# A second scalar operand for GpSimd's weight scalings in a two-block transformer kernel

## What is computed

```python
# swa: sliding window of 128 with sinks
e = jnp.exp(s - m)
p = e / (jnp.sum(e, axis=-1, keepdims=True) + jnp.exp(sk - m))
return jnp.einsum('bhgqk,bkhd->bqhgd', p.astype(v.dtype), vb)
...
# na: neighbourhood attention, 8 heads of 64, all 512 keys with a bias
s = jnp.einsum('brqhd,brkwhd->bhrqkw', q, k).astype(jnp.float32) + bias.astype(jnp.float32)
p = jax.nn.softmax(s.reshape(b, NA_HEADS, rows, GRID_W, kh * GRID_W), axis=-1)
...
# ca: cross attention, 4 heads of 128, 256 keys of a memory
s = jnp.einsum('bthd,bmhd->bhtm', q, kv[:, :, 0]).astype(jnp.float32)
p = jax.nn.softmax(s, axis=-1).astype(zq.dtype)
```

## Time and profile before

| | us |
|---|---|
| median of 3 runs | 2685.29 |
| the profiled execution, its own time | 2683.39 |
| its span | 2681.2 |
| PE busy | 2519.5 (94%) |
| DVE busy | 1330.3 (50%) |
| ACT busy | 715.8 (27%) |
| POOL busy | 1772.3 (66%) |

### The profile page before, as it was taken

One profiled execution on the slowest core, in us unless ns is written; L12 is line 12 of the kernel. 1 busy time (PEld: TensorE's weight loads), 2 busy tenths in 40 slices (PEclk: granted clock), 3 DMA queues, 4 the chain that ended last, 5 costly groups with the idle time before them and its releaser, 6 DMA issues. The chain is left out here.

```text
span 2681.2 us, 36597 instructions
## 1 busy us (share of the span) xinstructions
PE 2519.5 (94%) x11854; PEld 2038.9 (76%) x11854; DVE 1330.3 (50%) x2616; ACT 715.8 (27%) x1504; POOL 1772.3 (66%) x993
## 2 busy tenths in 40 slices
PE   8998889899999979899998999999999899999998
PEld 6786677588888767688886777777877777787877
DVE  6467886443342575411223566664138334751552
ACT  4305785301101263300112222222016232100002
POOL 4465455577777576577775544455779767687884
PEclk9998999999999989999999999999999999999999
DMA  7682001264563202233332311212423214233332
GB/s 262 188 232 72 1 1 39 94 206 153 176 194 94 63 17 91 74 98 94 96 100 71 102 56 57 62 56 66 108 83 71 82 50 123 79 105 91 89 104 75
DMA packets 420545, 259.73 MB, mean 97 GB/s; under 512 B 62844, under 2 KB 411513, under 8 KB 414017
## 3 DMA queue, kind: packets, MB, share of 16 engines
q1 hardware_dynamic: 395024, 199.47, 25.7%
q10 hardware_dynamic: 25393, 58.63, 6.6%
HBM read 253.86 MB, written 8.10 MB: 98 GB/s over the span
## 5 line engine op out<-in xcount | busy, mean ns | idle before, releaser
L677 POOL TENSOR_TENSOR W<-RAW,zeros 128x1024 fp32r<-128x1024 f32 (+2 forms) x349 | 668.2, 1915 | 657.8 <-PE PA L778 312.8
L684 POOL TENSOR_TENSOR W<-RAW,W 128x1024 fp32r<-128x1024 f32 (+2 forms) x355 | 849.1, 2392 | 49.2 <-ACT W L1543 19.4
L775 PE MATMUL PA<-H,W 128*128 128x512 f32 x1288 | 506.0, 393 | 7.7 <-DVEq L2412 2.3
L778 PE MATMUL PA<-H,W 128*128 128x512 f32 x1288 | 503.4, 391 | 0.0
L775 PE MATMUL PA<-A,W 128*128 128x512 f32 x944 | 373.9, 396 | 16.5 <-DVE A L2038 10.7
L778 PE MATMUL PA<-A,W 128*128 128x512 f32 x944 | 371.8, 394 | 0.0
L786 PE MATMUL PA<-H,W 128*128 128x512 f32 x1288 | 318.3, 389 | 0.0
L775 PEld LDWEIGHTS PA<-H,W 128*128 128x128 f32 x1288 | 242.3, 188 | 62.4 <-POOL W L677 7.4
L778 PEld LDWEIGHTS PA<-H,W 128*128 128x128 f32 x1288 | 242.4, 188 | 50.5 <-issue 0.5
L786 PEld LDWEIGHTS PA<-H,W 128*128 128x128 f32 x1288 | 241.7, 188 | 50.3
L786 PE MATMUL PA<-A,W 128*128 128x512 f32 x944 | 236.7, 393 | 0.0
(11 more groups left out here) (375 smaller groups left out, 3929.8 us busy)
## 6 DMA issues: line engine op xcount, KB each, us to landing
AD<-in_ada_w_dram ACTq DMA_DIRECT2D x40, 1024.0 KB, 5.1
RAW<-in_w_in_dram SPq DMA_DIRECT2D x160, 256.0 KB, 3.1
RAW<-in_mlp_w_up_dram SPq DMA_DIRECT2D x128, 256.0 KB, 3.0
RAW<-in_mlp_w_down_dram SPq DMA_DIRECT2D x128, 256.0 KB, 3.0
RAW<-in_w_up_dram SPq DMA_DIRECT2D x88, 256.0 KB, 3.1
RAW<-in_nsa_w_in_dram SPq DMA_DIRECT2D x40, 256.0 KB, 4.1
RAW<-in_w_down_dram SPq DMA_DIRECT2D x16, 384.0 KB, 3.4
RAW<-in_swa_w_in_dram SPq DMA_DIRECT2D x20, 256.0 KB, 3.3
```

The lines of the kernel that those rows point to most:

```text
L677: e.tensor_tensor(W[0][:, s, 0:kc], RAW[:, s, 0:kc], zeros[:, 0:1].rearrange("p (a b) -> p a b", b=1).broadcast_to([P, kc, P]), ALU.add).t ...
L684: e.tensor_tensor(W[1][:, s, 0:kc], RAW[:, s, 0:kc], W[0][:, s, 0:kc].bitcast(F32), ALU.subtract).then_inc(w_split, 1)
L775: pe.matmul(PA[s][:, 0:n], W[0][:, s, k], hi, start=(k == 0), stop=False)
L778: mm = pe.matmul(PA[s][:, 0:n], W[0][:, s, k], lo, start=False, stop=False)
```

## The change

Two instructions on GpSimd take another form; nothing else is touched, and no instruction is moved in any engine's order.

1. The scalings without a gate (`swa`, `na`, `ca`) multiply by the reciprocal and then by a second scalar operand, a column of the constant `ones`.
2. The high halves of the panels that are made between the scalings of `na` and `ca` (16 panels) are made by a `tensor_scalar` that adds a zero column twice as scalar operands, in place of the `tensor_tensor` addition of a broadcast column. The panels outside keep the `tensor_tensor`.

```diff
-        def split_hi(e, p, s, kc):
+        def split_hi(e, p, s, kc, filling=False):
             if not isinstance(p, int) or p >= 2:
                 e.wait_ge(w_hi_used, p - 1)
             e.wait_ge(w_loaded[s], ((p - s) * 16) + 32 if not isinstance(p, int) else (p // 2 + 1) * 32)
+            if filling:
+                e.tensor_scalar(W[0][:, s, 0:kc], RAW[:, s, 0:kc], zeros[:, 0:1], zeros[:, 0:1], ALU.add, ALU.add).then_inc(w_hi, 1)
+                return
             e.tensor_tensor(W[0][:, s, 0:kc], RAW[:, s, 0:kc], zeros[:, 0:1].rearrange("p (a b) -> p a b", b=1).broadcast_to([P, kc, P]),
                             ALU.add).then_inc(w_hi, 1)
...
                 elif grp["gate"] is None:
-                    pool.tensor_scalar(w, w, inverse, None, ALU.mult).then_inc(sem("scaled"), 1)
+                    pool.tensor_scalar(w, w, inverse, ones[:, 0:1], ALU.mult, ALU.mult).then_inc(sem("scaled"), 1)
...
                 if fills and i % plan.fill == plan.fill - 1:
-                    split_hi(pool, *fills[i // plan.fill])
+                    split_hi(pool, *fills[i // plan.fill], filling=True)
```

## The result

| | before | after |
|---|---|---|
| median of the runs | 2685.36 us (6 runs) | 2695.96 us (6 runs) |
| lowest and highest | 2681.62, 2686.85 | 2693.65, 2699.52 |
| profiled execution, its own time | 2683.39 | 2694.41 |
| its span | 2681.2 | 2692.2 |

The ratio is 1.0047, 95% interval 1.0036 to 1.0058: about 12.6 us slower (10.6 by the two medians, which lies inside the interval). The forecast was 2692.7 us, 7.4 slower, within 2681 to 2696. The direction was right, but the loss is larger than the sum: the median of 2695.96 is just inside the range, and 2685.3 x 1.0047 = 2697.9 us is above it.

What follows compares the result with a forecast made beforehand. The prediction took a loop of DVE and ACT to set `na`'s pace, with POOL beside it. Collisions +8.7 and tail -1.3, all else 0, gave +7.4 us: 2692.7 us, range 2681 to 2696.

Steps and rivals of the forecast that it cites:

- the tail: End of `na`: PE no longer waits for the last scaling; -1.3 us, bounds 0 to -2.
- Scalings at 0.77 us: The 112 scalings take 0.77 us instead of 1.87, which cuts 35 us of POOL's time in `na`.
- rival C: Second operand leaves scalings at 1.87 us, or `split_lo` stays where it is; nothing moves, 2685 us; chance 0.10.
- `split_lo` collides, 1.65 us per head: In `na`, `split_lo` starts 0.17 us before the queries' subtraction and blocks it, in six heads; +8.7 us in all.
- High halves: took 1.5 us, priced at 0: 16 high halves between scalings take 1.5 us, bounds 1.5 to 3.7; POOL done before the reciprocal in `na`; 0.
- rival D: PE's 2.3 us gap per head in `na` lets its clock fall; 1 us a head, 2699 us; chance 0.07.
- The first collision: First of six in `na`: only 0.4 us, since `split_lo` no longer holds up the bias by 1.25 us.
- `ca` and `swa` at 0: PE's waits there are not for POOL; 0 each, bounds -0.5 to +0.5 (`ca`), -0.5 to 0 (`swa`).
- Rival B: No collision in `na`: `split_lo` comes after the second keys' subtraction has begun, or DVE goes first; 2682 us, chance 0.17.

Runs made afterwards that it cites:

- the experiment on forms: Kernel before, with four forms of the scaling by turns in `swa` and three of the high half in `ca`; one execution 2682.72 us.
- halves by ones: Changed kernel with its high halves by two multiplications with ones instead of two additions of zero; 2692.23 us, ratio 1.0033 against the kernel before.
- the kernel with both parts and the wait: Changed kernel with `split_lo` in `na` waiting for the low half of the next head's keys; 2685.14 us, ratio 1.0004 against the kernel before.
- the kernel with the wait: Kernel before with the quick scalings, and `split_lo` in `na` waiting for the low half of the next head's keys; 2684.31 us, ratio 0.9991.
- the early `split_lo`: Kernel before with only `split_lo` in `na` moved one unit earlier, behind the scaling of unit 4h; 2697.40 us, ratio 1.0035.

## Why the forecast came out as it did

| part of `na`, us | before | scalings only | the change | forecast, difference |
|---|---|---|---|---|
| to head 1's queries | 6.76 | 7.78 | 7.79 | 0 |
| to head 2's | 10.45 | 10.53 | 10.53 | 0 |
| to head 3's | 12.06 | 12.74 | 13.58 | +0.4 |
| to head 7's | 47.76 | 54.23 | 56.46 | +6.6 |
| to the output projection | 24.81 | 24.38 | 26.46 | +0.35 |

(Heads are counted from 0; the forecast's five times 1.65 us are four in the fourth row and one in the last, there less the tail's 1.3. The differences of the change are +1.0, +0.1, +1.5, +8.7 and +1.7 us.)

- **Scalings at 0.77 us**: right, so rival C is out, and with them POOL's relief, though not its size. The window of the changed kernel's `na` (columns as in the earlier trace rows) has POOL busy for 72.59 of 104.5 us, where 88.30 of 93 stood and about 50 were forecast; the slow high halves take the rest. PE is busy for as long as before. That the relief buys PE nothing was read rightly from the earlier trace rows.

```profile
2002.00:2106.50 104.50, 86.36 (x486) 72.34 (x485) 88.24 (x163) 60.31 (x132) 72.59 (x47) 0.98 0.24 56
```

- **`split_lo` collides, 1.65 us per head**: right for the part that it was worked out for. The scalings alone lose 6.47 us over four heads, 1.62 each, in the subtraction and with the lead (0.20 us) that were named. For the Trainium skill (SBUF — State Buffer, § Who interferes with whom) this is the rule of the exclusive lock. For `tensor_tensor` the rows here agree: the subtraction grew from 0.69 to 2.75 us beside one of 2.40.
- **High halves: took 1.5 us, priced at 0.** This is the step that failed. It rested on the row of the gated scalings, two multiplications, as if the number of scalar operands made them quick; the experiment on forms shows that the operations do. At 3.81 us the half ends behind the reciprocal of unit 4h. The forecast said in its bounds what then follows: at 3.7 us `split_lo` comes to lie in the first subtraction for the keys, "with a loss like the one counted". That happened (2082.93, inside 2082.35 to 2083.5), yet the loss is larger than the one counted, by 0.55 us per head over four heads (8.70 instead of 6.47). The second keys lose to `split_lo` what the queries lost with the scalings alone (2.73 us instead of 0.69), and two scalings now lie beside the queries and the first keys as well. With the halves come 5.2 us of `na`'s +13.0: 0.8 in head 2, 2.2 in the four heads, and 2.1 in the last row, of which 1.6 are the clock (rival D, below). The bounds were worked out, but the upper one was then put at no cost in the sum, and the range ended at the forecast mechanism with the quick half.
- **The first collision (+0.4) and the tail (-1.3)**: with the scalings alone the first is +0.68. The last row is -0.43 where +0.35 was expected: head 7's collision costs 1.72 us (from the queries' start to the mask step 4.24 instead of 2.52), so the tail gives 2.15, more than its bound of 2. Against that stands 1.0 us at the start of `na` that nobody forecast (last section). That the scalings alone cost 7.8 us in `na`, near the sum of 7.4, is therefore partly luck.
- **`ca` and `swa` at 0**: right for `ca`; `swa` is 0.8 us shorter in the profiled execution, where 0 to 0.5 was allowed.
- **Rival B** would have needed `split_lo` behind the keys. Held there by a wait, the kernel gives 0.9991 where B had 2682 us. There the keys' subtractions take their bare 1.38 us and PE's waits for them 1.5 us in all, as B had it; B's condition was not met by the change.
- **Rival D** had the clock follow the longer gaps, at 1 us in each of six heads. The changed kernel has six gaps of 2.0 to 2.9 us. Behind five of them PE goes on at the higher level, and `na` was granted 0.98 on average, as before. Behind the last, in head 7, the clock fell: from 2086 to 2090 it shows 0.68. PE there, in the changed kernel and then with the scalings alone, where it did not fall:

```profile
2086.30 0.50 PE L1001 MATMUL PS<-KK1h,QS 128*128 128x512 f32 x1 [2.90 <-DVE KK1l L1965]
2086.87 2.25 PE L803 MATMUL PA<-H,W 128*128 128x512 f32 x6
```

```profile
2083.72 0.50 PE L998 MATMUL PS<-KK1h,QS 128*128 128x512 f32 x1 [0.82 <-DVE KK1l L1962]
2084.29 1.55 PE L800 MATMUL PA<-H,W 128*128 128x512 f32 x6
```

From these scores to the next PE takes 4.92 us (2086.30 to 2091.22) against 3.34 (2083.72 to 2087.06), and DVE then waits 0.92 us for PE. So D's mechanism occurs once and costs 1.6 us. The length of the gap does not decide alone: none of the others (2.92 us in head 4) brought a fall, nor did one of 2.37 us in head 7 with halves by ones, where the last row is 24.34 us; while with the scalings alone it fell behind two gaps of 1.98 and 1.96 us in the loop (2042.77 and 2069.98). There it can be hidden: head 6 takes 13.70 us from queries to queries with the fall, and 13.70 without one in the kernel with halves by ones.

The time of the whole change is thus a collision of 1.6 us per head, in six heads, that comes from the quick scalings and is made worse by the slow halves to 2.2, in one attention of 100 us in a kernel of 2,700; and, of `na`'s +13.0 us, 1.6 and 1.0 in which PE runs at the lower clock, in its last head and at its start.

## What to carry to other kernels

An engine that is made faster starts its next instruction earlier; before doing so, look up what will then be under way on the engine that shares a port with it. Here the quick scalings alone saved POOL 57 us (busy 1772.3 before, 1714.8 with them) and lost 8.6 us of time, and one wait that leaves POOL idle took the loss away. And take a duration only from a row with the same operations, not merely with the same number of operands and the same shape: a rewrite "with neutral second operand" can make an instruction twice as quick or half as quick.

## What the runs showed of the hardware

- **GpSimd's `tensor_scalar` depends on its operations.** By the difference between 1024 and 512 elements (means 2853 and 1572 ns for one addition; 3811 and 2074 for two; 1246 and 771 for two multiplications) an element costs 2.5, 3.4 and 0.93 ns. The Trainium skill (GPSIMD Engine Reference, § 3.1 and § 4.1) has bodies of one or two operations at 1.03 cycles an element, an estimate of 0.86 ns by the 1.2 GHz of its example; that is near the third figure alone, and the measurement decides.
- **What a `tensor_scalar` on GpSimd keeps from DVE is not its own duration.** Beside a scaling with one operand (1.81 us in the earlier trace rows) the subtractions with two SBUF inputs lost 0.39 us; beside one with two operands, up to 0.47 (the kernel with both parts and the wait). A `tensor_tensor` of 2.40 us that had begun 0.20 us ahead of one cost it 2.06 us. The other way round, a scaling that starts beside DVE's bias addition takes 1.86 us instead of 0.77 (2069.31 in the kernel with the wait).
- **TensorE's clock comes back later in the first microseconds of `na`, and I can't say why.** After the gap of 4.17 us the second scores' matmuls take 0.40 us in the kernel before, with the halves only, with the early `split_lo` and in the comparison of forms, and 0.63 us, the lower level, in all seven profiled executions with quick scalings in `na`. It costs 1.0 us (6.76 against 7.8 us up to head 1's queries). It can't be the scalings of `na` themselves: the first of them starts only at 1999.62 in the kernel before, and the matmul of 1998.08 was already at the higher level. No run here tells what it is. From 1996 to 2000 the changed kernel is granted 0.66 and the kernel before 0.76, although the changed kernel's scores had begun 1.45 us earlier (1993.19 and 1994.64):

```profile
1996.00:2000.00 4.00, 4.00 (x15) 3.17 (x14) 1.44 (x5) 3.11 (x6) 0.38 (x1) 0.76 0.00 0
```

```profile
1996.00:2000.00 4.00, 4.00 (x14) 3.16 (x13) 0.78 (x3) 2.97 (x7) 0.77 (x1) 0.66 0.00 0
```

(Windows of the kernel before and of the changed one: length, busy us of PE, PEld, DVE, ACT, POOL, then PEclk.)
